# Third feed-forward layer by chunks, its gated tiles turned by VectorE: one edit to a two-block fp32 transformer kernel on Trainium2

## What is computed

```
x = x + 0.5 * swiglu(rms_norm(x, ffn1_norm), ffn1_wg, ffn1_wu, ffn1_wd)      # third feed-forward layer, "f2"
h = rms_norm(x, mix_norm); x = x + concat(o_nsa(h), o_sb(h)) @ w_out
x = x + memory_cross_attention(rms_norm(x, mem_x_norm), rms_norm(mem, mem_kv_norm), wq, wk, wv, wo, g_q, g_k)
x = x + 0.5 * swiglu(rms_norm(x, ffn2_norm), ffn2_wg, ffn2_wu, ffn2_wd)      # fourth feed-forward layer, "f3"
```

## Time and profile before

| | us |
|---|---|
| median of three runs | 1176.64 (1176.08 to 1177.44) |
| the profiled execution | 1176.4 |
| its span, first to last instruction | 1174.6 |
| TensorE busy (matmul) | 1160.7 (99%) |
| VectorE busy | 842.7 (72%) |
| ScalarE busy | 598.5 (51%) |
| mean granted TensorE clock | 1.000 |

### The profile page before, as it was taken

How to read it: one execution, slowest core, us unless ns; L and a number is a source line. 1 busy time by engine, 2 the same in 40 slices (tenths; PEclk the granted TensorE clock), 3 DMA queues, 4 the chain that set the end, 5 groups by cost and what they waited for, 6 DMA issues and landing times.

```text
span 1174.6 us, 15455 instructions
## 1 busy us (share of the span) xinstructions
PE 1160.7 (99%) x6009; PEld 968.7 (82%) x6009; DVE 842.7 (72%) x1438; ACT 598.5 (51%) x797; POOL 60.2 (5%) x109
## 2 busy tenths in 40 slices
PE   9999999999999999999999999999999999999998
PEld 7888888888879988888887888888898787888887
DVE  6666577988757768798885675445558877979874
ACT  7744454554345555454444464424467866545441
POOL 1100010000000000000001500000110001000000
PEclk9999999999999999999999999999999999999999
DMA  8744536555444443655543665455355142565540
GB/s 288 287 156 162 206 118 236 216 215 213 174 151 178 147 142 144 244 221 215 188 175 123 232 229 203 174 221 199 105 208 210 37 144 73 186 245 215 215 143 37
DMA packets 34690, 213.58 MB, mean 182 GB/s; under 512 B 4665, under 2 KB 6841, under 8 KB 10041
## 3 DMA queue, kind: packets, MB, share of 16 engines
q1 hardware_dynamic: 34617, 212.59, 49.1%
HBM read 211.53 MB, written 1.05 MB: 181 GB/s over the span
## 4 chain that ended last, share of the span: by engine, by line
PE 94%; DVE 2%; ACT 1%; DMA 1%; issue 1%; SPq 0%; POOL 0%; DVEq 0%; ACTq 0%; POOLq 0%
PE ps L325 29%; PE ps L327 29%; PE ps L326 29%; PE ps L331 3%; DVE wlo L1559 1%; PE ps L797 1%; DMA raw<-in_w_v 1%; PE ps L848 1%; PE ps L669 1%; ACT whi L1086 1%; PE ps L825 0%; PE ps L649 0%; DVE tmp L1578 0%; PE ps L772 0%; ACT xThi L1107 0%
## 5 line engine op out<-in xcount | busy, mean ns | idle before, releaser
L1559 DVE TENSOR_TENSOR wlo<-raw,whi 128x2048 fp32r<-128x2048 f32 (+2 forms) x196 | 432.9, 2233 | 65.5 <-ACT whi L1086 65.5
L1086 ACT ACTIVATE whi<-raw 128x2048 fp32r<-128x2048 f32 (+2 forms) x196 | 363.0, 1868 | 125.7 <-DMA raw<-in_w_gu 68.7
L325 PE MATMUL ps<-whi,xThi 128*128 128x512 f32 (+2 forms) x960 | 373.0, 389 | 1.5 <-DVE wlo L1559 0.8
L327 PE MATMUL ps<-whi,xTlo 128*128 128x512 f32 (+2 forms) x960 | 370.7, 386 | 0.0
L326 PE MATMUL ps<-wlo,xThi 128*128 128x512 f32 (+2 forms) x960 | 370.4, 386 | 0.0
L325 PEld LDWEIGHTS ps<-whi,xThi 128*128 128x128 f32 x960 | 180.3, 188 | 39.9 <-DVE wlo L1559 2.5
L327 PEld LDWEIGHTS ps<-whi,xTlo 128*128 128x128 f32 x960 | 180.3, 188 | 36.5
L326 PEld LDWEIGHTS ps<-wlo,xThi 128*128 128x128 f32 x960 | 180.4, 188 | 35.0
L1691 DVE STREAM_TRANSPOSE f_sil<-f_hid 32x128 f32<-32x128 f32 x480 | 145.3, 303 | 10.0 <-DVE f_hid L1683 0.9
L1201 ACT ACTIVATE f_sil<-ps,stats 128x256 f32<-128x256 f32 x88 | 40.7, 470 | 214.6 <-PE ps L327 213.8
L325 PE MATMUL ps<-whi,f_hThi 128*128 128x512 f32 x352 | 139.9, 398 | 0.0
(11 more groups left out here) (289 smaller groups left out, 1181.2 us busy)
## 6 DMA issues: line engine op xcount, KB each, us to landing
raw<-in_w_gu SPq DMA_DIRECT2D x88, 1024.0 KB, 4.9
raw<-in_w_dn SPq DMA_DIRECT2D x44, 1024.0 KB, 5.5
raw<-in_w_u SPq DMA_DIRECT2D x8, 1024.0 KB, 5.5
raw<-in_w_ao SPq DMA_DIRECT2D x8, 1024.0 KB, 5.1
raw<-in_w_v SPq DMA_DIRECT2D x6, 1024.0 KB, 4.9
raw<-in_w_bv SPq DMA_DIRECT2D x4, 1024.0 KB, 5.0
raw<-in_w_bk SPq DMA_DIRECT2D x4, 1024.0 KB, 4.8
raw<-in_w_bq SPq DMA_DIRECT2D x4, 1024.0 KB, 4.9
```

Of the source, the lines that this page charges most:

```text
L325: e.matmul(ps, a[0], b[0], start=start, stop=False)
L327: return e.matmul(ps, a[1], b[0], start=False, stop=stop)
L1086: e.activation(dst[:, cs], raw_cols(i, cs), ACT.Copy).then_inc(*inc("whi", i, p))
L1559: e.tensor_tensor(lo[:, cs], raw_cols(i, cs), hi[:, cs].bitcast(F32), ALU.subtract).then_inc(*inc("wlo", i, p))
```

## The change

- f2 goes by chunks like the others. The 40 TensorE transposes of its chunks 0 to 9 go; 160 VectorE block transposes come.
- The three calls of TensorE's `mem_keys` at chunks 2, 3, 4 and the one at 6 stand between down(c-1,0) and down(c-1,1), as before with one turn fewer ahead of them. Memory tiles and keys are turned into banks 2 and 3, with fewer waits.
- ScalarE's `hi(c,0)` and `hi(c,1)` stand together, ahead of `beside(c)`. VectorE's low parts likewise, and its norm of the memory keys moves from chunk 4 to chunk 5.
- In every layer by chunks, the last chunk's single unit is split ahead of the high parts on ScalarE, and between the two low parts on VectorE.

```diff
@@ tensor: ffn @@
-            if S == "f2":
-                by_tiles()
-            else:
-                by_chunks()
+            project(("gu", S, 0, 1), GB[1], half_of(xT, 1), pair, normed=(S, 1), last=True)
+            for c in range(1, FFN_CHUNKS):
+                pair[:] = [take(), take()]
+                for t in range(2):
+                    e.wait_ge(*at("hid", S, c - 1, t))
+                    if hook and c == MEM_CHUNK + 1:
+                        e.wait_ge(*at("vm", t))
+                    project(("gu", S, c, t), GB[t], half_of(xT, t), pair, last=t)
+                dn = [take()]
+                for t in range(2):
+                    if c == FFN_CHUNKS - 1:
+                        turn_hid(c, t)
+                    downs(c - 1, t, dn)
+                    if hook and not t:
+                        hook(c)
@@ tensor: mem_keys @@
-            banks = XB[1], GB[0]
             for t in range(2):
                 e.wait_ge(*at(f"mem{t}"))
-                e.wait_ge(*at("hidlo", "f2", t + 1, 1))
+                if t:
+                    e.wait_ge(*at("xmul", "mem", 0, 1))
                 for h in range(2):
-                    turn(banks[h], [memx[t][:, 512 * h + 128 * i:512 * h + 128 * i + 128] for i in range(4)], "x", "mem", t, h)
+                    turn(XB[h], [memx[t][:, 512 * h + 128 * i:512 * h + 128 * i + 128] for i in range(4)], "x", "mem", t, h)
...
-            e.wait_ge(*at("hidlo", "f2", 5, 1))
@@ scalar: ffn @@
-                    e.wait_ge(*(at("hid", S, c - 1, t) if S == "f2" else at("hidlo", S, c - 1, t)))
+                    e.wait_ge(*at("hidlo", S, c - 1, t))
...
-                blocks = S != "f2" and c < FFN_CHUNKS - 1
+                blocks = c < FFN_CHUNKS - 1
...
-            at_chunk(0, True)
-            if S == "f2":
-                for c in range(FFN_CHUNKS):
-                    if c:
-                        gated(c, 0)
-                        hi(c - 1, 1)
-                    gated(c, 1)
-                    hi(c, 0)
-                    at_chunk(c, False)
-                hi(FFN_CHUNKS - 1, 1)
-                return
+            split()
             for c in range(FFN_CHUNKS):
                 if c:
                     gated(c, 0)
                 gated(c, 1)
-                ahead = 2 if c < FFN_CHUNKS - 1 else 0
-                split(min(ahead, counts[c]))
+                ahead = min(counts[c], 2)
+                split(ahead)
                 for t in range(2):
                     hi(c, t)
-                split(max(counts[c] - ahead, 0))
+                if beside:
+                    beside(c)
+                split(counts[c] - ahead)
@@ vector: ffn @@
                 if c < FFN_CHUNKS - 1:
                     turn_hid(c)
-                for t in range(2):
-                    lo(c, t)
-                left = min(counts[c], 2) if c < FFN_CHUNKS - 1 else 0
-                split(counts[c] - left)
+                lo(c, 0)
+                if c == FFN_CHUNKS - 1:
+                    split(counts[c])
+                lo(c, 1)
+                if beside:
+                    beside(c)
+                left = min(counts[c], 2)
+                if c < FFN_CHUNKS - 1:
+                    split(counts[c] - left)
@@ vector: beside @@
-            if c in (2, 3, MEM_CHUNK, MEM_CHUNK + 2):
+            if c in (2, 3, MEM_CHUNK + 1, MEM_CHUNK + 2):
                 next(keys)
```

More of the change, by code:

```diff
@@ L709, in mem_keys @@
             yield
-            e.wait_ge(*at("hidlo", "f2", 5, 1))
             for t in range(2):
                 e.wait_ge(*at("mkn", t))
-                turn(banks[t], [kv[t][:, 128 * i:128 * i + 128] for i in range(2)], "km", t)
+                turn(XB[t], [kv[t][:, 128 * i:128 * i + 128] for i in range(2)], "km", t)
             yield
@@ L1192, in gmlp, with ffn @@
             split(2)
-        def ffn(S, at_chunk, second, counts=None):
+        def ffn(S, second, counts, beside=None):
             def gated(c, t):
@@ L1501, in to_mem @@
                 scaled_hi("f3", 1, h)
[L1503 to L1511, removed]
         gmlp()
         enter("f0", "g")
-        ffn("f0", lambda *_: split(), lambda: enter_second("f0", "g"), [3, 4, *[3] * 8, 1])
+        ffn("f0", lambda: enter_second("f0", "g"), [3, 4, *[3] * 8, 1])
         attention()
         enter("f1", "a")
-        ffn("f1", lambda *_: split(), lambda: enter_second("f1", "a"), [3, 4, *[3] * 8, 1])
+        ffn("f1", lambda: enter_second("f1", "a"), [3, 4, *[3] * 8, 1])
         split()
@@ L1678, in gmlp, with ffn @@
             split()
-        def ffn(S, at_chunk, counts=None):
+        def ffn(S, early, counts, beside=None):
             def gated(c, t):
@@ L1694, in lo @@
             def lo(c, t):
-                src = sil[t][:, :] if S != "f2" and c < FFN_CHUNKS - 1 else PS[XB[t]][:, 0:256]
+                src = sil[t][:, :] if c < FFN_CHUNKS - 1 else PS[XB[t]][:, 0:256]
                 evac_lo([flat(a) for a in hT[t]], src, "hidhi", "hidlo", S, c, t)
             gated(0, 0)
-            at_chunk(0, True)
-            if S == "f2":
-                for c in range(FFN_CHUNKS):
-                    if c:
-                        gated(c, 0)
-                        lo(c - 1, 1)
-                    gated(c, 1)
-                    lo(c, 0)
-                    at_chunk(c, False)
-                lo(FFN_CHUNKS - 1, 1)
-                return
+            early()
             for c in range(FFN_CHUNKS):
@@ L1857, in mem_keys @@
         def mem_keys():
-            banks = XB[1], GB[0]
             for t in range(2):
-                scaled("mem", t, banks, gain(8), mT)
+                scaled("mem", t, XB, gain(8), mT)
                 yield
@@ L2103, in to_mem @@
             scaled("f3", 1, DB[0], gain(9))
[L2105 to L2114 removed]
         gmlp()
         enter("f0", "g", DB, gain(3), late=split)
[L2118 removed]
+        ffn("f0", split, [3, 4, *[3] * 8, 1])
         attention()
         enter("f1", "a", ((0, 1), (4, 5)), gain(4), spare=DB[1])
[L2121 removed]
+        ffn("f1", lambda: split(2), [3, 4, *[3] * 8, 1])
         gg = stat("gg", n=8)
@@ L2136, in beside, with early @@
                 mixer_angles()
-        def chunk_f2(c, start):
-            if start:
-                whiten(1)
-            chunks(2, [3, *[3] * 9, 1], beside)(c, start)
-        ffn("f2", chunk_f2)
+        def early():
+            whiten(1)
+            split(2)
+        ffn("f2", early, [3, *[3] * 9, 1], beside)
         mixer()
         to_mem()
-        ffn("f3", lambda *_: split(2), [3, 4, *[3] * 7, 1, 0])
+        ffn("f3", lambda: split(2), [3, 4, *[3] * 7, 1, 0])
         for t in range(2):
```

63 lines of the change are left out of this document (5 added, 58 removed).

## The result

The changed kernel takes 1179.75 us (median of 12 runs, 1179.01 to 1180.80), the kernel before, timed beside it, 1177.66 (12 runs, 1176.08 to 1180.14). The ratio is 1.0017, with a 95% interval of 1.0009 to 1.0025: slower, by some 2 us. The profiled execution took 1180.8 us with a span of 1178.9.

A forecast was written before the change was run, and what follows sets the result against it. TensorE's own list of work plus its gaps was taken as the bound. 1176.4 - 5.1 (transposes) - 3.9 (layer ends) + 10.9 (ring) + 2.6 (clock) = 1180.9, with the median offset 1181.1 us; range 1177.8 to 1185.2.

The forecast's parts named there:

- the ring: f2, chunk 4: ScalarE's memory copies wait behind down(3,1) while TensorE's gu(5,0) waits for them; 10.9 us added.
- the change without the ring: Faster rival: ScalarE makes the copies during TensorE's projections, so gains stand alone, 1167.6 us; covered ring 0.12, 0.10 of it faster.
- The price without the landing: Chunk 4 rival: unit 128 landed earlier, gap 5.2 us, result 1175.4, no difference; chance 0.02.
- The clock after the gap: Behind the chunk 4 gap TensorE's granted clock falls and coming back costs 2.6 us, bounds 0 to twice that.
- Transposes off TensorE: f2, chunks 0 to 9: four turns per chunk leave TensorE, 0.51 us each chunk, 5.1 us less.
- The rival of the whole duration: f2's transposes cost TensorE their full 0.272 us each, 10.9 us instead of 5.1, giving 1175.3; chance 0.02.
- VectorE at 0: f2's 160 block transposes, 48.5 us, hide in VectorE's idle time and cost 0; bounds 0 to 5 us.
- my rival: VectorE falls behind in f2's chunks 1 to 4, 2 to 5 us on top, 1183 to 1186; chance 0.10.
- The sign I named for chunks from 6 on: f2: f_hid of the second token tile would come every 16.32 us from chunk 6 on if the forecast was right.
- The last chunk of f2 at 0: Moving the last chunk's unit in f2 was counted at 0, as no wait stands there.
- Ends of f0 and f1 at -3.9: Earlier splitting of the last unit removes both TensorE waits around the sums into x, 3.9 us; bounds 0 to 3.9.
- The median against the profiled execution: The median of the runs was put 0.24 us above the profiled execution, taking the sum 1180.9 to 1181.1.

The follow-up runs named there:

- 1: `copies_and_unit_early`: changed kernel with ScalarE's memory copies ahead of high part (4,1) and VectorE's unit 125 ahead of low part (4,1): 1167.10 us, ratio 0.9908.
- 9: `late_and_ahead`: changed kernel with TensorE's memory projections behind down(3,1) and ScalarE's memory copies ahead of units 127 and 128: 1166.72 us, ratio 0.9906.
- 2: Changed kernel with only VectorE's low part of unit 125 moved ahead of low part (4,1), ScalarE's order left: 1173.36 us, ratio 0.9964.
- 3: Changed kernel with 44 extra unread matmuls of 512 columns filling TensorE's gap ahead of gu(5,0): 1177.91 us, ratio 1.0000.
- last_chunk_only: Kernel before with only the last chunk's unit split ahead of the high parts in f0, f1 and f3, f2 by tiles: 1172.06 us, ratio 0.9951.
- 7: Changed kernel with only ScalarE's memory copies moved, between high parts (4,0) and (4,1), or just ahead of units 127 and 128: 1170.52 and 1170.36 us.
- 10: The kernel of 9 with the last chunks' unit put back behind the high and low parts, f2's too: 1174.11 us, ratio 0.9965.
- experiment 4: `last_chunk_only`: kernel before with only the last chunk's unit split ahead of the high parts in f0, f1 and f3: 1172.06 us, ratio 0.9951.
- 5: Kernel before, unchanged, run again for a second trace: 1179.27 us.
- 6: Kernel before with extra unread matmuls filling TensorE's two waits for the sums into x: 1180.33 us with 18 at each place, 1177.41 with 9.
- waits_filled: Kernel before with 18 extra unread matmuls of 128 columns ahead of each of two waits for the sums into x: 1180.33 us, ratio 1.0022.
- copies_ahead: Changed kernel with only ScalarE's memory copies moved between high parts (4,0) and (4,1), VectorE's order left: 1170.52 us, ratio 0.9934.

## Why the prediction was right, and where it was not

The time lies in the range, the sign is the forecast one, and the mechanism is shown: opening the ring alone makes the change a gain (1, 9). The fastest kernel, at 1166.7, is close to where the prediction put the change without the ring (1167.6). The size was 2.1 us where 4.5 were forecast. (Numbers in brackets below are experiments.)

- **The ring: right to 0.1 us in the profiled execution.** Forecast steps at 0.2, 0.65, 1.0, 3.3, 8.2, 10.05, 10.4 and 10.9 us after down(3,1); counted from 719.04 they were 0.26, 0.70, 1.05, 3.36, 8.27, 10.08, 10.44 and 11.0. That it is this close is partly luck: the landing alone had bounds of 3.5 to 9.4, and the one that was traced took 4.91, the median. The price without the landing, 5.2 forecast in the rival, was 5.1 counted from starts, a wait of 4.94 (2).
- **The clock after the gap: right in kind, somewhat too high.** 2.6 forecast; the 48 matmuls of gu(5) took 13.15 us instead of 10.88, so 2.3, and filling the gap gave 1.84 (3). The source of the 2.6 is weak. The distances at the start of the program are there, but the profile's clock doesn't show the lower level beside them (third from last):

```profile
2.00:4.00 2.00, 2.00 (x10) 2.00 (x11) 0.00 (x0) 0.20 (x1) 0.00 (x0) 1.00 0.84 229
```

  The 2.6 also compared turns of tiles (0.21 us apart) with passes of other matmuls (0.10). That the lower level was at work there, as the title of those rows has it, isn't shown; the 1.7 to 2.8 us behind the gaps of these experiments are.
- **Transposes off TensorE: right.** 10 x 0.51 = 5.1 forecast. `copies_and_unit_early` and `last_chunk_only` differ in f2 alone, by 1172.06 - 1167.10 = 4.96 us on the same chip, and the first of them still had its 0.6 us of wait. The rival of the whole duration would have given 10.9 and is out. The rule in "VectorE: DVE Perf Modes", "Rules for kernel authors", of the Trainium skill gives a 128 x 128 transpose to TensorE where the result may lie in PSUM. The measurement decides against it for this edit: 16 block transposes of 0.3 us do the work of TensorE's four turns, and with idle time on VectorE they win.
- **VectorE at 0: right for the change, but not for the reason given.** It is busy for 79% of f2, as forecast, and TensorE doesn't wait for it. But the edit does delay VectorE at chunk 4, which the prediction had not counted, and the gap hid that. With the gap gone it shows, 0.6 us (1) to 2.5 us (7), at the last chunk and not at chunks 1 to 4, where my rival had put it; with the order at chunk 4 mended as well it is 0 again (9). The sign I named for chunks from 6 on, `f_hid` every 16.32 us, was wrong: VectorE came late to it at chunks 6, 7 and 9 and wrote it at uneven distances, while TensorE kept 16.32. `late_and_ahead`, which has no debt, is late at the same three chunks, so catching up isn't the reason; VectorE's other work stands right ahead of `f_hid` there (low parts of units, at chunk 9 also the small work on the positions).
- **The last chunk of f2 at 0: wrong.** "No wait stands there" was read from f2 by tiles. By chunks there would be one of 1.9 us (10); the change avoids it. No error of the sum, but of its working: a wait that the new order would bring and the same edit takes away.
- **Ends of f0 and f1 at -3.9: the term that was too small.** The waits are gone, as forecast (-1.98 and -2.27 in the traces). But the part alone gave 5.4 us in the median (4). The step that failed is the sentence "the longest gap now is 2.1 us, and the granted clock is 1.00 throughout". One trace showed 1.00. In 10 of the 15 runs timed beside experiment 4 the mean clock is below 1.000, and the second trace shows it at 0.50 behind those same waits (5). So these waits cost up to 3 us more in many executions, and the edit takes that too. Of the 1.5 us by which the term was too small, some 0.3 is the counting of waits from the ends of matmuls, and 1.2 is the distance between the median of the kernel before and those of its runs that kept a clock of 1.000 (1177.49 - 1176.30). How much of the 1.2 is the clock isn't settled: with the waits filled and the clock up in all runs the median fell by only 0.76, within its interval around nothing (6). The term makes 1.5 of the 2.4 us by which the forecast was off; 0.8 is the clock's price behind the gap (2.6 - 1.84).
- **The median against the profiled execution.** I put it 0.24 us above. With more runs it stands 1.3 above (1177.66 against 1176.4), since the profiled execution was one in which the clock stayed up.

## What to carry to other kernels

When an in-order engine's instruction is moved ahead of another, follow its wait to the engine that ends it: if that engine's next work needs anything that now stands behind the moved instruction, the two wait for each other in turn, however short the pieces, and everything queued between (a split, a DMA issue, a landing) is added to the price. Short waits of TensorE (here 1.9 and 2.1 us) may cost more than their length, and not in every execution, so read the mean clock of all runs before taking one profile for the median. A gap also hides debts: after it is closed, look for what had caught up in it.

## What the runs showed of the hardware

- The granted clock fell to 0.50 behind waits of TensorE of 3.25, 4.94 and 10.84 us and stayed at 1.00 behind one of 1.3 us. Behind two of 1.87 and 2.07 us it fell in one trace of the kernel before and stayed up in the other. In the three gaps traced the price didn't grow with the length: 2.8 us on the 48 matmuls after 3.25 us, 1.7 after 4.94, 2.3 after 10.84.
- Keeping TensorE busy with matmuls whose result nobody reads held the clock: mean 1.000 instead of 0.995, and 1.84 us less in spite of 44 extra matmuls.
- A float32 matmul of 128 columns between other such ones took 0.22 us (4.02 us for 18 from start to start, `waits_filled`), two records each.
- A transfer of 1 MB issued right behind four small loads landed after 8.5 us (`copies_ahead`), one issued with a pause of 0.9 us behind them after 5.95 (`late_and_ahead`); the median of such transfers was 4.9.
